# Second mixer of a two-block transformer kernel: rotary rows by transfers inside SBUF, indexer first, attention in pairs of heads with half product tiles between, gates by tanh

## The chip, the cores and the metric

One core of a Trainium2 chip runs the whole program in one launch. The time is the device time of one execution in microseconds. A core has TensorE (PE, matrix products into PSUM; PEld is its weight load), VectorE (DVE), ScalarE (ACT), GpSimd (POOL) and SyncE (SP, which only issues transfers here). PSUM has eight banks of 128 partitions by 512 fp32.

## The reference, cut to what matters

512 tokens of width 1024 in fp32 go through two blocks. The change touches only the mixer of the second block:

```python
def hybrid_mixer(xn, w_in, pool_w, pool_scale, w_pool_proj, w_attn_proj, w_out):
    proj = xn @ w_in
    u_pool, q, k, v, iq, ik, iw, gates = jnp.split(proj, cuts, axis=-1)
    pooled = multiscale_pool(u_pool)     # causal means over 2, 4, 8, 16 tokens, minus the token
    mixed = jnp.einsum('bsgc,gcd->bsgd', pooled, pool_w).reshape(B, S, POOL_WIDTH) * pool_scale
    y_pool = mixed @ w_pool_proj
    q, k, iq, ik = (rope_partial(a, pos) for a in (q, k, iq, ik))   # first 16 of 64 dims turned
    o = indexed_sparse_attention(q, k, v, iq, ik, iw)
    y_attn = o @ w_attn_proj
    g = jax.nn.sigmoid(gates).reshape(B, S, 2, D_MODEL)
    return (g[:, :, 0] * y_pool + g[:, :, 1] * y_attn) @ w_out

def indexed_sparse_attention(q, k, v, iq, ik, iw):     # per block row of 128 queries
    s = relu(iq . ik over 8 index heads of 64) / 8;  score = sum_h iw[h] / sqrt(8) * s[h]
    keep the 128 best causal keys of each query; softmax(q . k / 8) over them, times v, 8 heads of 64
```

After it come the conv FFN of the second block and the final norm, unchanged.

## The kernel before, in words

The program is written engine by engine (`nc.Block`), with semaphores; on each engine the order of the source is the order of the run. All products are made at fp32 accuracy out of fast matmuls: each weight unit of 128 x 2048 is split into a high part (ScalarE, `split`, L672) and a low part (`lo`: VectorE L1640, or GpSimd L585), and each product is three matmuls (L1153 to L1155). A product tile with 1024 inner values ("dense tile") is 24 matmuls of 512 columns, one with 512 inner values (`yp`, `ya`) is 12. Weight units pass through two slots in the order of `U`: SyncE loads unit u once unit u-2 has been parted, ScalarE splits it once TensorE has used unit u-2, VectorE or GpSimd then makes the low part, and TensorE waits for that (`weights_ready`).

PSUM tiles are handed out ahead of time by `Tiles.take`: each set of banks is a ring of its own (`GEMM` is banks 0 to 3, `AUX` 4 to 6, `HOLD` 7), and `wait_free` makes TensorE wait until the tile that had the bank before has been read.

The second mixer on TensorE: four pool tiles; the sum of squares for the norm (`rstd`, needed by everyone who reads a tile); q, k (column tiles), v (token tiles), iq, ikw, with after each pair of q, k, iq tiles two `swap` matmuls (L1530) that exchange the rotary halves of a copy of the tile (ScalarE L719 copies, GpSimd L643 multiplies by the cosines, VectorE L2164 and L2167 multiply by the sines and add); `project_pooled` (L1539) after the first q unit; `indexer(qt)` for block rows 1, 2, 3 (L1566, eight heads each of 64 rows; ScalarE L1062 takes the relu out of the bank, VectorE L2207 and L2209 weigh and sum) with gate units `gp` between; `yp` (products of the pooled branch, whose readers L1886 wait for the sigmoid gates, L1066). VectorE finds the 128 best keys by 16 rounds of eight maxima and a replacement (`top_rounds`, L2221, L2222): those of block rows 1 and 2 in one run after their indexer, those of 3 one per head in attention.

Attention then goes head by head over n = 0 to 31: `scores` (L1590), `turn_weights` of head n-1 (L1230), `weigh_values` of head n-2 (L1605), and in the first 16 steps a whole tile of the second gate (`ga`) at each odd n. On VectorE `at_maximum` (L2242, L2244) adds the mask and takes the row maximum; it may write `at_s[:, n % 2]` only when head n-2 has been turned. ScalarE takes the exponentials (L1087) and copies the turned weights (L1095). When the eight heads of a block row are done, `at_scaled` (VectorE L2251, L2254) divides, TensorE turns the rows, ScalarE (L1112) and VectorE (L2264, `at_lo`) make the high and low parts for `ya`. The attended rows of a block row (`o`) lie in bank 7 or bank 3, in turn. `ya`, `merged_hi`/`merged_lo` and `wo2` follow.

Of the kernel before, what the change touches and what calls it, by code (L numbers as in the profile page):

```python
# [8 lines left out]
ALU = mybir.AluOpType  # L9
# [45 lines left out]
for _g, _group in enumerate(VECTORS):  # L55
    _r = 0
    for _name, _n in _group:
# [5 lines left out]
          ("block_causal", P), ("chunk_of", CPT), ("rope_swap", P), ("pool_count", POOL_G * 16),  # L63
# [11 lines left out]
def shape_constants():  # L75
# [24 lines left out]
    c, s, swap = np.ones((P, S)), np.zeros((P, S)), np.zeros((P, P))  # L100
    for base in (0, HD):
        c[base:base + half] = c[base + half:base + rot] = cos
        s[base:base + half], s[base + half:base + rot] = -sin, sin
        for d in range(half):
            swap[base + d + half, base + d] = swap[base + d, base + d + half] = 1.0
    put("rope_cos", c)
    put("rope_sin", s)
    put("rope_swap", swap)
# [46 lines left out]
def program(nc, A, out):  # L155
# [10 lines left out]
    with ctx:  # L166
# [112 lines left out]
        pool_t, pooled = area(0, 3, 16 + S), area(1584, POOL_G, S)  # L279
        iq, ik = area(4096, 4, S), area(6144, S)  # L280
        at_q, at_k, at_v = area(R, 4, S), area(R + 2048, 4, S), area(R + 4096, TT, S)
# [57 lines left out]
        for name, n in [("sc", 3), ("conf", 2), ("ifa", 1), ("ml", 4), ("gate3", 4), ("y3", 1), ("gla", 4),  # L339
                        ("gate2", 4), ("y2", 1), ("gate0", 4), ("y0", 1), ("gate1", 4), ("y1", 1),  # L340
                        ("wo", 4), ("up1", FT), ("down1", FT // 2),
                        ("pool", 2), ("q", 2), ("k", 2), ("v", 2), ("iq", 2), ("ikw", 1), ("gp", 4), ("yp", 2),
# [17 lines left out]
        HEADS = TT * NH2  # L360

        def out_step(n):

            qt = (n - NH2 - 3) // NH2
            return qt if n >= NH2 + 3 and (n - NH2 - 3) % NH2 == 0 else None

        def ga_step(n):
            return n // 2 if n < 16 and n % 2 else None


# [62 lines left out]
        take("pl", AUX, POOL_G)  # L433
        take("rope", AUX, 13)
        take("iwT", AUX)
        take("idx", AUX, 3 * NH2)
        for name in ("gp", "yp"):
            take(name, GEMM, 8)
        take("ga", GEMM[:3], 8)
        take("o", HOLD + GEMM[3:], TT)  # L440
        for n in range(HEADS + 4):
            if n < HEADS:
                take("s", AUX)
            if 1 <= n <= HEADS:
                take("pt", AUX)
            if out_step(n) is not None:
                take("oT", AUX)
# [215 lines left out]
        def _(act):  # L663
# [349 lines left out]

            split(U["q"] + 1)
            rn = [0]

            def rotary():

                n = rn[0]
# [1318 lines left out]
```

## Time and profile before

| | us |
|---|---|
| median of 3 runs (lowest, highest) | 1784.95 (1782.24, 1785.29) |
| the profiled execution | 1785.4 |
| its span, first to last instruction | 1783.6 |
| TensorE busy, mean granted clock | 1675.6 (94%), 0.96 |
| VectorE, ScalarE, GpSimd busy | 950.0, 666.7, 325.3 |
| share of TensorE in the chain that ended last | 80% |

A row of a list or a timeline has the line, the engine, the operation, what it writes and reads, and its shape; "busy" on TensorE counts records that overlap, since matmuls are pipelined, so the step from one start to the next is the better price of a matmul. The granted clock is given as a share of 2.4 GHz.

### The profile page before, as it was taken

Reading aid. Unit: us, or ns where it says so; the run is one execution under the profiler, and the core shown is the slowest. Engines: PE = TensorE matmul, PEld = TensorE weight load, DVE = VectorE, ACT = ScalarE, POOL = GpSimd, SP = SyncE. Lnnn points to the kernel's source line nnn. Section 1 sums busy time; section 2 is a strip of 40 time slices with the busy share of each in tenths; the row PEclk is TensorE's granted clock in tenths of the full one; section 3 lists DMA queues with packets and bytes.
Section 4 is the critical chain, followed back from the end, with each engine's and each line's share of the span. In section 5 each row is a group of like instructions: output and inputs, shape, how many; then the busy total and the mean of one; then the engine's idle time right before and its main releaser. Section 6 shows DMA issues by size and latency. Waiting matters only on the chain.

```text
span 1783.6 us, 20062 instructions
## 1 busy us (share of the span) xinstructions
PE 1675.6 (94%) x7618; PEld 1333.8 (75%) x7618; DVE 950.0 (53%) x1274; ACT 666.7 (37%) x804; POOL 325.3 (18%) x150
## 2 busy tenths in 40 slices
PE   5899999989899799999998899998999999999997
PEld 4687678768777488888887668666767788888886
DVE  4549545436896644445333854664435455556333
ACT  2333353233223444444223422234353444544322
POOL 0320014224334011111000121343313211111000
PEclk8799999989999899999999999899999999999999
DMA  8323213206572133333222131221202233333221
GB/s 288 97 73 95 67 52 95 71 25 205 186 246 71 29 107 101 94 94 94 96 100 87 65 95 56 88 76 48 71 6 89 83 94 94 95 101 110 95 94 47
DMA packets 190956, 168.58 MB, mean 95 GB/s; under 512 B 9158, under 2 KB 180718, under 8 KB 190766
## 3 DMA queue, kind: packets, MB, share of 16 engines
q1 hardware_dynamic: 173485, 148.49, 27.0%
q10 hardware_dynamic: 16800, 16.83, 2.9%
q0 software_dynamic: 608, 2.41, 0.4%
q8 instruction: 42, 0.69, 0.2%
q14 instruction: 21, 0.16, 0.0%
HBM read 165.61 MB, written 2.10 MB: 94 GB/s over the span
## 4 chain that ended last, share of the span: by engine, by line
PE 80%; DVE 12%; issue 3%; ACT 2%; SPq 1%; DMA 1%; POOL 0%; DVEq 0%; ACTq 0%
PE bank L1153 23%; PE bank L1155 23%; PE bank L1154 23%; DVE work L1680 3%; PE bank L1178 1%; SPq L236 1%; DVE work L1743 1%; DVE w_lo L1640 1%; PE bank L1160 1%; PE bank L1161 1%; PE bank L1162 1%; PE bank L1230 1%; DVE tbuf L1652 1%; PE bank L1400 1%; PE bank L1566 1%
## 5 line engine op out<-in xcount | busy, mean ns | idle before, releaser
L1153 PE MATMUL bank<-h_hi,w_hi 128*128 128x512 f32 x1536 | 613.6, 399 | 29.4 <-DVE h_lo L1658 13.3
L1155 PE MATMUL bank<-h_hi,w_lo 128*128 128x512 f32 x1536 | 604.0, 393 | 0.0
L1154 PE MATMUL bank<-h_lo,w_hi 128*128 128x512 f32 x1536 | 603.9, 393 | 0.0
L1153 PEld LDWEIGHTS bank<-h_hi,w_hi 128*128 128x128 f32 x1536 | 291.8, 190 | 113.9 <-issue 37.5
L672 ACT ACTIVATE w_hi<-w_raw 128x2048 fp32r<-128x2048 f32 x131 | 250.2, 1910 | 303.3 <-PE bank L1155 234.3
L1640 DVE TENSOR_TENSOR w_lo<-w_raw,w_hi 128x2048 fp32r<-128x2048 f32 x88 | 202.5, 2301 | 262.6 <-ACT w_hi L672 262.3
L1155 PEld LDWEIGHTS bank<-h_hi,w_lo 128*128 128x128 f32 x1536 | 291.9, 190 | 62.0
L1154 PEld LDWEIGHTS bank<-h_lo,w_hi 128*128 128x128 f32 x1536 | 292.3, 190 | 59.9 <-issue 1.2
L585 POOL TENSOR_TENSOR w_lo<-w_raw,w_hi 128x2048 fp32r<-128x2048 f32 x43 | 204.1, 4746 | 467.3 <-ACT w_hi L672 467.3
L1153 PE MATMUL bank<-y_hi,w_hi 128*128 128x512 f32 x480 | 193.9, 404 | 19.4 <-DVE work L1886 8.5
L1154 PE MATMUL bank<-y_lo,w_hi 128*128 128x512 f32 x480 | 191.1, 398 | 0.0
L1155 PE MATMUL bank<-y_hi,w_lo 128*128 128x512 f32 x480 | 191.0, 398 | 0.0
L621 POOL TENSOR_TENSOR work<-work 128x512 f32 x44 | 56.8, 1292 | 468.0 <-ACT work L975 468.0
L1153 PEld LDWEIGHTS bank<-y_hi,w_hi 128*128 128x128 f32 x480 | 93.2, 194 | 42.7 <-DVE tbuf L1886 9.1
L1680 DVE SCALAR_TENSOR_TENSOR work<-work,small 128x256 f32<-128x256 f32 x154 | 108.8, 707 | 5.5
L1154 PEld LDWEIGHTS bank<-y_lo,w_hi 128*128 128x128 f32 x480 | 93.1, 194 | 19.8 <-issue 0.5
L1155 PEld LDWEIGHTS bank<-y_hi,w_lo 128*128 128x128 f32 x480 | 92.7, 193 | 20.0
L2067 DVE SCALAR_TENSOR_TENSOR work<-bank,par,work 128x511 f32<-128x511 f32 (+1 forms) x88 | 61.7, 743 | 71.1 <-ACT work L969 71.1
L969 ACT ACTIVATE work<-work,par 128x512 f32<-128x512 f32 x44 | 35.8, 815 | 97.8 <-DVE work L2056 97.8
L969 ACT ACTIVATE work<-bank,par 128x512 f32<-128x512 f32 x44 | 30.0, 683 | 105.2 <-PE bank L1155 105.2
L2067 DVE SCALAR_TENSOR_TENSOR work<-work,par 128x511 f32<-128x511 f32 (+1 forms) x88 | 61.9, 745 | 10.1 <-ACT work L969 10.1
L719 ACT ACTIVATE work<-bank,par 128x512 f32<-128x512 f32 x32 | 21.9, 686 | 116.8 <-PE bank L1155 116.8
(250 smaller groups left out, 1516.9 us busy)
## 6 DMA issues: line engine op xcount, KB each, us to landing
w_raw<-in_w_in SPq DMA_DIRECT2D x94, 512.0 KB, 4.6
w_raw<-in_ffn_w_up SPq DMA_DIRECT2D x44, 512.0 KB, 4.6
w_raw<-in_w_up SPq DMA_DIRECT2D x44, 512.0 KB, 4.5
work<-in_ada_w ACTq DMA_DIRECT2D x16, 1024.0 KB, 7.6
w_raw<-in_ffn_w_down SPq DMA_DIRECT2D x22, 512.0 KB, 3.9
w_raw<-in_w_down SPq DMA_DIRECT2D x22, 512.0 KB, 3.6
work<-in_ada_w SPq DMA_DIRECT2D x8, 1024.0 KB, 12.2
w_raw<-in_w_o SPq DMA_DIRECT2D x8, 512.0 KB, 4.0
```

The lines of the kernel that those rows point to most:

```text
L236: eng.dma_start(ada_place(n), A["ada_w"][0][:, n * 2 * P:(n + 1) * 2 * P].rearrange("(k p) n -> p k n", p=P))\
L585: pool.tensor_tensor(w_lo[u % 2][:, :], raw[u % 2][:, :], w_hi[u % 2][:, :].bitcast(FP32), ALU.subtract)\
L621: pool.tensor_tensor(work[:, bass.ds(i * (2 * S) + k * S, S)], cbuf[:, k, 0, :], cbuf[:, k, 1, :], ALU.mult).then_inc(sem("hid" + n), 1)
L672: act.activation(w_hi[u % 2][:, :], raw[u % 2][:, :], ACT.Copy).then_inc(hi_done, 1)
L719: release(act.activation(dst, src, func, **kw), t)
L969: act.activation(cbuf[:, k, part, :], src, ACT.Identity, scale=par[:, bass.ds(i * 2 + at, 1)], **kw).then_inc(sem("center" + n), 1)
L1153: pe.matmul(dst, w_hi[s][:, at:at + n], hi, start=first, stop=False)
L1154: pe.matmul(dst, w_hi[s][:, at:at + n], lo, start=False, stop=False)
L1155: return pe.matmul(dst, w_lo[s][:, at:at + n], hi, start=False, stop=last)
L1640: dve.tensor_tensor(w_lo[u % 2][:, :], raw[u % 2][:, :], w_hi[u % 2][:, :].bitcast(FP32), ALU.subtract)\
L1680: ins = dve.scalar_tensor_tensor(out=unit[:, 0, :], in0=unit[:, k, :], scalar=c_act[:, k:k + 1], in1=unit[:, 0, :], op0=ALU.mult, op1=ALU.add)
L2067: ins = dve.scalar_tensor_tensor(out=c[:, back:S], in0=src[:, 0:S - back], scalar=w, in1=c[:, back:S], op0=ALU.mult, op1=ALU.add)
```

## The change

It does five things, all in the second mixer.

1. **Rotary.** The swap matmuls, the copies to `tbuf` and GpSimd's products with the cosines go. VectorE reads each q, k, iq, ik tile out of its bank times `rstd` straight into place (`heads_out`). SyncE then gathers the 16 turning rows of each head into an area `turned` of 128 partitions x 512 by four transfers inside SBUF (`rotary_out`, 64 KB each read or written), VectorE turns all of them with four operations (`rotate`: two of 64 partitions, two of 128), and four transfers bring them back (`rotary_back`). Transfers stand in SyncE's queue among the weight loads.
2. **Order.** The order of units becomes pool, iq, ikw, q, k, v, gp, yp, ga, ya. All four pool tiles are read first; iq's tiles use the `GEMM` ring behind them. The indexer is cut into 12 pairs of heads, one after each of the tiles q1 to q3, k0 to k3, v0 to v3 and gp0; `project_pooled(g)` follows k0 to k3. `v` is read by ScalarE.
3. **Top-k spread.** Rounds of block rows 1 and 2 stand between index sums, the rest of 2 and all of 3 in attention steps 0 to 10.
4. **Attention in pairs.** A step m takes the scores of heads 2m and 2m+1, a half product tile, the turns of pair m-1, a half tile, the values of pair m-2. The 36 half tiles are gp 2 to 7, yp 0 to 7 (each one half), ga 0 to 7. Scores, turned weights and turned outputs share the ring of banks 3 to 6; `o` has bank 7 alone; gate and pool products use banks 0 to 2.
5. **Gates.** `tanh(x/2)` in the same table as the exponential; the readers add 1, and `wo2` is scaled by 0.5.

The core of the diff (helpers `ACT`/`POOL` order, tables of `take` and the copies of `split`/`lo` cut where the text above says them):

```diff
-        take("q", AUX[1:], 2)
-        for name, n in (("q", 2), ("k", 4), ("v", 4), ("iq", 4), ("ikw", 1)):
+        for name, n in (("iq", 4), ("ikw", 1), ("q", 4), ("k", 4), ("v", 4)):
             take(name, GEMM, n)
...
-        take("o", HOLD + GEMM[3:], TT)
+        for name in ("gp", "yp", "ga"):
+            take(name, GEMM[:3], 8)
+        take("o", HOLD, TT)
+        for m in range(PAIRS + 3):
+            if m < PAIRS:
+                take("s", GEMM[3:] + AUX, 2)
+            if 1 <= m <= PAIRS:
+                take("pt", GEMM[3:] + AUX, 2)
+            if m in O_TURNED_AT:
+                take("oT", GEMM[3:] + AUX)
...
+        O_TURNED_AT = (10, 11, 15, 18)
...  SyncE
+            rotary_out("iq", iq, T["iq"][3])
+            rotary_out("ik", ik, T["ikw"][0])
+            cols(U["k"], w2, KT, C_K, 2 * P)
+            rotary_back("iq", iq)
+            rotary_back("ik", ik)
...  TensorE
+                if p == 0:
+                    pe.wait_ge(sem("iq_back"), 64)
+                    pe.wait_ge(sem("ik_back"), 64)
...
+            for m in range(PAIRS + 3):
+                if m < PAIRS:
+                    scores(2 * m)
+                    scores(2 * m + 1)
+                if m <= PAIRS:
+                    fill_part(2 * m)
+                if 1 <= m <= PAIRS:
+                    turn_weights(2 * m - 2)
+                    turn_weights(2 * m - 1)
+                if m <= PAIRS:
+                    fill_part(2 * m + 1)
+                if 2 <= m <= PAIRS + 1:
+                    weigh_values(2 * m - 4)
+                    weigh_values(2 * m - 3)
+                if m == PAIRS + 1:
+                    fill_part(2 * m)
+                if m in O_TURNED_AT:
...
+                if m == PAIRS + 2:
+                    fill_part(2 * m - 1)
...  VectorE
+            for c in (2, 3):
+                heads_out("iq", c, iq, 1.0)
+            lo(U["q"])
+            t = T["ikw"][0]
+            wait_full(dve, t)
+            for b in (0, HD):
+                ins = dve.tensor_tensor(ik[b:b + HD, :], bank[t.bank][0:HD, :], rstd[0:HD, :], ALU.mult)
+            dve.wait_ge(sem("iw_rows"), 1)
+            release(ins, t)
+            dve.wait_ge(sem("rope_in"), 16)
+            rotate("iq")
+            lo(U["q"] + 1)
+            rotate("ik")
+            window_mean(3)
+            heads_out("q", 0, at_q, HEAD_SCALE)
...
+            ROUNDS_AT = {0: (2, 3), 1: (2, 3), 2: (2, 2), **{m: (3, 2) for m in range(3, 11)}}
+            for m in range(PAIRS + 3):
+                if m < PAIRS:
+                    at_maximum(2 * m)
+                    at_maximum(2 * m + 1)
+                if 7 <= m <= 10:
+                    for c in (2 * m - 14, 2 * m - 13):
+                        opened("yp", c, merged[:, c, :])
+                if m in ROUNDS_AT:
+                    top_rounds(*ROUNDS_AT[m])
+                if m >= 6 and (m - 6) % 4 == 0:
+                    at_scaled((m - 6) // 4)
+                if m in O_TURNED_AT:
+                    at_lo(O_TURNED_AT.index(m))
```

ScalarE in step m: the two exponentials, at even m the split of the weight unit due in two steps, the copies of the turned pair, one raw gate tile, one gate opened. GpSimd: the low parts from v's second unit on, and the scaling of each gate tile by `rstd`.

## Rows read from the trace of the kernel before

**Rows 1.** Busy time by stretch (x records), granted clock, transfers: indexer, attention, whole stage.
```profile
core 0: us, PE busy (x) PEld busy (x) DVE busy (x) ACT busy (x) POOL busy (x), PEclk, DMA share, GB/s
1130.80:1191.76 60.96, 60.81 (x241) 44.42 (x241) 49.67 (x124) 22.29 (x35) 28.66 (x12) 0.94 0.22 70
...
1221.70:1329.79 108.09, 100.82 (x513) 73.49 (x512) 49.95 (x158) 45.42 (x113) 28.50 (x12) 1.00 0.12 40
...
1008.16:1329.79 321.63, 300.36 (x1392) 226.38 (x1391) 171.59 (x365) 108.53 (x193) 87.99 (x41) 0.96 0.20 62
```

**Rows 2.** Waits of TensorE, 1008 to 1357: total, times, longest in us.
```profile
PE bank L1153 <- DVE work L1886: 4.9, 1, 4.9
PE bank L1539 <- DVEq L2157: 4.6, 1, 4.6
PE bank L1230 <- ACT work L1087: 4.4, 8, 1.3
...
PE bank L1530 <- ACT tbuf L1049: 1.9, 1, 1.9
PE bank L1566 <- DVE work L2167: 1.7, 1, 1.7
PE bank L1153 <- DVE y_lo L2264: 1.4, 1, 1.4
```

**Rows 3.** Timeline of TensorE around two swaps: start, length, instruction.
```profile
1105.22 2.04 PE L1530 MATMUL bank<-tbuf,cst 128*128 128x512 f32 x4
1106.69 0.79 PE L1153 MATMUL bank<-h_hi,w_hi 128*128 128x512 f32 x1
1107.32 0.40 PE L1154 MATMUL bank<-h_lo,w_hi 128*128 128x512 f32 x1
1107.55 0.40 PE L1155 MATMUL bank<-h_hi,w_lo 128*128 128x512 f32 x1
```

**Rows 4.** Timeline at the first index heads of block row 3, and their window.
```profile
1185.72 0.39 PE L1155 MATMUL bank<-h_hi,w_lo 128*128 128x512 f32 x1
1186.04 1.13 PE L1566 MATMUL bank<-work 64*128 64x512 f32 x4
...
1186.00:1187.00 1.00, 0.96 (x4) 0.49 (x5) 1.00 0.87 304
```

**Rows 5.** Timeline of TensorE, a head's scores of 512 columns.
```profile
1308.10 1.12 PE L1590 MATMUL bank<-work 64*128 64x512 f32 x2
1309.15 0.66 PE L1230 MATMUL bank<-cst,work 128*128 128x128 f32 x4
```

**Rows 6.** Timeline of VectorE in attention, 256 columns of scores, block row 3's rounds.
```profile
1253.16 0.42 DVE L2242 CUSTOM_DVE_ANT_0 work<-bank,work 128x256 f32<-128x256 f32 x1 [4.18 <-issue]
...
1253.70 0.68 DVE L2221 MAX8 small<-sq 128x8 f32<-128x512 f32 x1
...
1255.20 0.42 DVE L2242 CUSTOM_DVE_ANT_0 work<-bank,work 128x256 f32<-128x256 f32 x1
...
1257.49 0.69 DVE L2254 TENSOR_TENSOR tbuf<-bank,small 128x512 f32<-128x512 f32 x1
```

**Rows 7.** Timeline of VectorE: the first pool tile read, and four products out of banks.
```profile
1008.99 0.69 DVE L2133 TENSOR_TENSOR work<-bank,rstd 128x512 f32<-128x512 f32 x1 [4.47 <-issue]
...
1207.02 2.48 DVE L1886 SCALAR_TENSOR_TENSOR work<-bank,work 128x512 f32<-128x512 f32 x4 [12.79 <-ACT work L1066]
```

**Rows 8.** Transfers: issues, size, median us to landing; and two issues in SyncE's timeline.
```profile
work<-in_ada_w SPq DMA_DIRECT2D x8, 1024.0 KB, 12.2
...
w_raw<-in_w_in SPq DMA_DIRECT2D x1, 64.0 KB, 2.6
...
1004.55 0.92 SPq L485 DMA_DIRECT2D w_raw<-in_w_in  x2
```

**Rows 9.** Windows as in rows 1: a stretch with one wait of TensorE; after 4.9.
```profile
147.18:155.00 7.82, 6.09 (x51) 6.08 (x51) 7.82 (x11) 2.40 (x2) 0.00 (x0) 1.00 0.43 134
1206.83:1213.64 6.81, 5.78 (x14) 4.56 (x15) 2.77 (x5) 4.97 (x9) 2.72 (x1) 0.50 0.45 138
```

**Rows 10.** Group of GpSimd's low parts, 1008 to 1410: count, busy, mean ns.
```profile
L585 POOL TENSOR_TENSOR w_lo<-w_raw,w_hi 128x2048 fp32r<-128x2048 f32 x16 | 74.2, 4636 | 129.5 <-ACT w_hi L672 129.5
```

More of the change, by code:

```diff
@@ L99, in shape_constants @@
     cos, sin = np.cos(ang).T, np.sin(ang).T
[L100 to L108, printed above, removed]
+    row = np.arange(P)
+    dim, second = (row % 32) // 4, row >= HD
+    put("rope_cos", cos[dim])
+    put("rope_sin", np.where(second[:, None], -sin[dim], sin[dim]))
     t = np.arange(16)
@@ L357, in program, with fill @@
         GATE2_AFTER = {0: 0, 1: 1, 2: 2, 3: 3, 5: 5, 6: 6}
[L360 to L368, printed above, removed]
+        PAIRS = TT * NH2 // 2
+        INDEX_PAIRS = [(qt, h) for qt in range(1, TT) for h in range(0, NH2, 2)]
+        def fill(f):
+            if f < 12:
+                return "gp", 2 + f // 2, 4 * (f % 2)
+            if f < 20:
+                return "yp", f - 12, 0
+            return "ga", (f - 20) // 2, 4 * (f % 2)
+        O_TURNED_AT = (10, 11, 15, 18)
         READ_FIRST = (7, 0, 1, 2, 3, 4, 5, 6)
@@ L551, in _, with rows_between @@
             ffn_units("1", A["ffn_w_up"][0], A["ffn_w_down"][0])
-            for name, c0 in (("pool", C_POOL), ("q", C_Q), ("k", C_K), ("v", C_V), ("iq", C_IQ)):
-                column_units(name, w2, c0, 2)
-            cols(U["ikw"], w2, KT, C_IK, IKW)
-            column_units("gp", w2, C_GATE2)
+            def rows_between(name, X, gather):
+                for half in range(2):
+                    for hh in range(2):
+                        rows = X[hh * HD + half * 8:hh * HD + half * 8 + 8]
+                        at = half * HD + hh * 32
+                        if name == "ik":
+                            if gather:
+                                dst, src = turned[name][at:at + 32, :], rows.unsqueeze(1).broadcast_to([8, 4, S])
+                            else:
+                                dst, src = rows, turned[name][at:at + 32:4, :]
+                        else:
+                            dst, src = (turned[name][at:at + 32, :], rows) if gather else (rows, turned[name][at:at + 32, :])
+                        sp.dma_start(dst, src).then_inc(sem(f"{name}_{'out' if gather else 'back'}"), 16)
@@ L1114, in _ @@
+            open_gate("ga", KT - 1)
             split(U["ya"] + 1)
-            for cc in range(KT):
-                open_gate("ga", cc)
             split(U["ya"] + 2)
@@ L2226, in _ @@
             ch.link(dve.tensor_copy(masks[0], const("causal_qk")))
-            indexer(1)
-            top_rounds(1, 0, TOPK // 8)
-            indexer(2)
-            top_rounds(2, 0, TOPK // 8)
-            indexer(3)
-            gated("yp", first=True)
+            lo(U["iq"] + 1)
+            window_mean(0)
+            window_mean(1)
+            for c in range(2):
+                heads_out("iq", c, iq, 1.0)
+            lo(U["ikw"])
+            window_mean(2)
+            for c in (2, 3):
+                heads_out("iq", c, iq, 1.0)
@@ L2234, in at_maximum @@
+            for p in (8, 9, 10, 11):
+                index_sum(p)
+                top_rounds(2, 2)
             def at_maximum(n):
```

461 lines of the change are left out of this document (234 added, 227 removed).

## The prediction

> **What bounds the kernel now.** I read the page's busy table first, where TensorE stands far ahead of every other engine, then the windows by stage [rows 1]: the second mixer, up to its last product stage, runs from 1008.16 to 1329.79, 321.6 us; TensorE is busy for 300.4 of it at a mean granted clock of 0.96. VectorE has 171.6, ScalarE 108.5, GpSimd 88.0. So this is TensorE's queue, and a change can save there matmul time, waits, or slow clock. The list of waits says who ends them [rows 2]: 4.6 us for the pooled rows, 1.9 and 1.7 at the last rotary swap, 4.9 before the pool products (their banks are freed by products that wait for sigmoids), 4.4 in eight pieces for attention's exponentials, 1.4 for the last attended rows. The last rows say what a wait costs beyond itself: after the 4.9 the granted clock is 0.50 (1.2 GHz) for 6.8 us, while a stretch with one wait of 1.7 (147.2 to 148.9, busy 6.1 of 7.8) stayed at 1.00 (2.4 GHz) [rows 9]. Half of the busy time at 0.50 is lost, 2.9 us there; clock losses below are counted so, from the windows behind each wait.
>
> **Removed.** *Swaps.* Two swaps take TensorE from 1105.22 to 1106.69, and the next dense matmul lasts 0.63 instead of 0.23: 1.87 for two [rows 3]; 13 swaps are 12.2 us. A dense tile of 24 matmuls at that step of 0.23 (0.2275 over a whole tile) is 5.46, its half 2.73.
> *Waits of the projections.* The pooled rows are used 50 us later than they are ready: 4.6, plus 0.8 behind it for a weight part and some 3.1 of half clock. The swap's chain goes: 3.6, plus 1.4 of clock on the dense work behind it. Together 13.5.
> *Index heads.* The indexer's window of 60.96 us [rows 1] holds eight gate tiles (43.7) and 1.4 of slow clock in them: 24 heads cost 15.8. The window 1186.00 to 1187.00 holds four matmul records of 64 rows, two whole heads in 0.96 [rows 4]: neighbours sit in opposite halves of the array and run side by side. Only the first pair of a run can now, since three banks are then emptied one by one (15.8 for 24 is 0.66 a head). In pairs, with a dense tile in which ScalarE empties banks, I take 1.06, 0.85 and 0.63 a pair by width: 10.2 in all, 5.6 saved.
> *Pool products' wait.* The first half of them now stands between pairs; 4.9 and 2.9 of clock go: 7.8.
> *Attention's waits.* Two dense half tiles per pair now cover maximum and exponential: the 4.4 go, and 0.2.
> *Head pairs.* A lone head of 512 columns takes 1308.10 to 1309.15, 1.05 [rows 5]; two are 2.1 against 1.06 side by side. Saved 1.04 at 512, and, scaled with the columns, about 0.83, 0.63 and 0.42: four pairs of each, 11.7.
> Removed in all: 12.2+13.5+5.6+7.8+4.6+11.7 = 55.4.
>
> **Added.** *The first wait.* q's first tiles had banks of their own. Now iq takes the ring of four, and counted through the takes its first tile falls on bank 3, the pool tile that VectorE empties fourth. rstd is there at 1008.99, where VectorE starts the first; four such operations in a row take 2.48 [rows 7]. TensorE starts at 1011.6 instead of 1008.16: 3.4, and 2.2 of clock. 5.6.
> *Index transfers.* Before the first index pair stands: ikw tile read by VectorE (two operations, 1.4), gather of ik, the rotation of iq (2.9), a low part (2.3), the rotation of ik (2.9), transfer back. Counted from iq's first tile: ikw's tile full 27.3, read 28.7, iq turned 31.6, low part 33.9, ik turned 36.8. No row shows a transfer inside SBUF. The nearest is the one of 64 KB, 2.6 to landing; the longest on this queue is 12.2 [rows 8]. I take 2.6 because 64 KB is exactly the size, and 1.3 for the three issues ahead of the last (0.46 each): back at 40.7. TensorE asks at 38.8: 1.9 of wait, 0.9 of clock. The gather is covered by the rotation of iq and the low part; q's and k's come 25 us and more before use. Behind the waiting SyncE stand the weights of k, needed 15 us later.
> *VectorE in attention.* This I think the change overlooks. at_maximum(2m) waits until the weights of the pair before are turned, and that lies between the two half tiles of step m. From there VectorE needs 0.54 a head at 256 columns (start to start), about 0.67 at 384; a top-k round at 512 is 1.50, a product from a bank 0.69 (0.60 in a row), scaling with its reciprocal 1.0 [rows 6]. Two places hang on what it does next. (a) yp takes three banks, so the half tile after the turn at m=7, 8, 9 (yp 3, 5, 7) needs the product of yp 0, 2, 4 read in that same step: 1.2+0.7 after the turn, 1.45+0.7 at 384. Waits of 1.7, 1.9, 1.8. (b) "o" now has bank 7 alone, and the values of the next block row wait for at_scaled, which stands behind the rounds: at m=6 1.2+3.0+1.0 against a cover of 3.2, 2.0 of wait; at m=10 1.45+1.3+3.0+1.0 against 3.3, 3.5. At m=14 there are no rounds and the cover holds. Five waits, 10.9. Clock: the rows at hand show it kept after 1.7 and lost after 4.9 [rows 9]; I charge 4.5, between nothing and 8.5 (1.7 each).
> *More changes of kind.* From the last dense start before them to the index heads it is 0.32 instead of 0.23 [rows 4], and about as much on the way back: 0.16 a change with return. 28 more in attention, 12 in the projections: 6.4. The Trainium skill, "TensorEngine Tiling (Array Packing)", section "Tiling Modes", speaks against the change here: it says that switching the tiling mode drains the engine, and 64-row pairs between 128-row tiles switch each time. Taken as a full drain both ways (0.39 recorded less 0.23 step, twice) that would be 12.8, 6.4 us more than the sum.
> *The end.* The last gate half is copied, another gate is opened and the attended rows are copied on ScalarE, then VectorE takes the low part: 0.6+0.6+0.6+0.7 and signals, 2.75, against 1.4 now [rows 2] and the scaling of the last block row (1.0), which a half tile will hide. GpSimd's low parts of 4.64 [rows 10] for gate unit 3 and the first pool unit come 0.5 before they are asked for; each is queued behind a gate scaling. I put 0.8 on these and the value step at m=17: 1.1 in all.
> Added in all: 5.6+2.8+15.4+6.4+1.1 = 31.3.
>
> At nothing: DVE in the index stage. Its queue (17 tiles read, seven low parts, the rotations, the index sums, 16 rounds for block row 1 and 8 for 2) fits, since its rounds end at 122.5 and the first maximum is asked at 124; if that cover were gone, each late microsecond would be paid in full. GpSimd loses its 13 rotations and stands nowhere else on the path. From the "ya" products on nothing changes.
>
> **Sum.** 55.4 - 31.3 = 24.1 faster. The profiled execution took 1785.4 (span 1783.6), 0.45 over the median 1784.95. 1785.4 - 24.1 - 0.45 = 1760.9, said as **1761**.
>
> **Rivals.** *Nothing waits for VectorE in attention* (the banks are free in time, or other slack absorbs it): 15.4 come back, 1745.5. For: VectorE is busy 50 of 108 us in attention [rows 1]. Against: the order within a step is fixed.
> *The clock falls each time and longer, the waits lengthen*: five times 3.1 instead of 4.5 is 11, the transfer's wait 2 more: 1774.
> *The pairs don't run side by side* (so part of the change doesn't do what it says): 11.7 and 5.6 are lost: 1778. Against: the four records in 0.96 us [rows 4].
> *Slower, by the transfers:* out and back stand in series before the first index pair. With 12.2 for each, 19.2 are added: 1780. It decides from 14.6 us a transfer (24.1 = 2 x 12); at 18 each it is 1792. For: thirty-two rows of 2 KB go to as many partitions behind 1 MB of weights on one queue. Against: weights of 512 KB land in the order of 4 to 6 us.
> The skill's rule of the drain, as a mechanism of this kernel: 1767, inside the forecast's own range.
>
> **How the numbers follow.** Forecast 0.50, with its own range 1753 to 1769; nothing waits for VectorE 0.13; clock and longer waits 0.17; no pairs 0.08; transfers up to the neighbourhood of no change 0.04, beyond it 0.08. A difference under 0.2% (3.6 us) can't be told from no change in this kernel. Faster 0.50+0.13+0.17+0.08 = 0.88, of which I give 0.02 to "same", as couplings between five queues were judged: 0.86; same 0.06; slower 0.08. The range leaves out the transfers' slow end and the deepest gain: 1744 to 1778.
>
> **What would show it.** Swaps gone and TensorE's busy time in the second mixer about 20 us lower; its first wait of 3 to 4 us before iq, ended by a VectorE product out of a bank; a wait under 3 us at the first index pair ended by a transfer; 64-row records two at a time in attention; waits of about 2 us before the fourth, sixth and eighth pool products and before the first values of block rows 1 and 2 (2 and 3.5 us), all ended by VectorE; no wait for exponentials. The prediction is wrong if that first index wait is over 5 us, if waits appear in every step rather than in five, or if GpSimd's low parts end waits of more than 2 us.

## The result, and the profile after

The changed kernel takes 1757.9 us (1755.7 to 1759.9, four runs) against 1785.1 for the kernel before, measured beside it: a ratio of 0.984, 95% interval 0.983 to 0.986. The forecast was 1761, within 1744 to 1778. Its profiled execution took 1757.8 us, with a span of 1756.0.

The stage that the prediction works on ran from 1008.16 to 1329.79 before, 321.6 us [rows 1]. Windows of the changed kernel, first that stage, then the stretches around four of its waits; the columns are those of rows 1:

```profile
core 0: us, PE busy (x) PEld busy (x) DVE busy (x) ACT busy (x) POOL busy (x), PEclk, DMA share, GB/s
1007.02:1305.33 298.31, 274.39 (x1365) 216.43 (x1364) 160.82 (x359) 105.21 (x192) 75.62 (x28) 0.96 0.24 73
1050.90:1053.31 2.41, 0.00 (x2) 0.03 (x1) 2.16 (x6) 0.00 (x0) 0.00 (x0) 1.00 0.24 51
1053.31:1060.00 6.69, 6.69 (x32) 5.03 (x32) 4.76 (x7) 2.46 (x3) 0.00 (x0) 1.00 0.48 155
1183.04:1191.82 8.78, 6.35 (x21) 4.93 (x21) 2.19 (x5) 2.64 (x5) 3.36 (x2) 0.61 0.01 2
1215.44:1225.00 9.56, 7.48 (x38) 5.84 (x38) 5.27 (x14) 2.35 (x6) 0.00 (x0) 1.00 0.12 43
1228.54:1243.03 14.49, 7.39 (x26) 5.59 (x26) 7.45 (x10) 2.71 (x4) 4.50 (x1) 0.65 0.24 72
```

The stage is 298.3 us long, 23.3 less. TensorE's busy time in it fell by 26.0 (300.4 to 274.4); the mean granted clock is the same 0.96. So the gain is work taken out of TensorE's queue, and not waiting. The rest of the 27.6 between the two profiled executions lies outside: 1.1 ahead of the stage, where nothing was changed, and 3.1 behind it, where before has three stretches of 3.4 us at 0.50 and after has one.

TensorE's waits of over 1 us in the stage and just behind it, as total, times, longest; what answers to [rows 2]:

```profile
PE bank L1634 <- DVE tbuf L2327: 9.5, 2, 7.1
PE bank L1187 <- DVE work L2347: 6.2, 3, 2.2
PE bank L1187 <- DVE work L2171: 3.3, 1, 3.3
PE bank L1187 <- DVE h_lo L2033: 2.7, 1, 2.7
PE bank L1187 <- DVE y_lo L2337: 2.5, 1, 2.5
PE bank L1578 <- issue: 2.4, 1, 2.4
```

Of the old waits of over 1 us one is left: the one for the low part of the last attended rows, before the attention projection (L2337 is `at_lo`), was 1.4 and is 2.5. New are 3.3 at the first iq tile (L2171 reads the pool tile), 2.4 at the first index pair, three of about 2 before pool products (L2347 opens the tile whose bank they need), and two before the values of a new block row (L2327 is `at_scaled`). The fourth line, L2033, lies behind the stage and was there before too (2.7 at 1353.4). No line names ScalarE's exponentials. What ended the wait that is put down to "issue" shows in the same list, in the weight load of that matmul:

```profile
PEld bank L1578 <- DMA work<-work: 2.8, 1, 2.8
```

The pairs, on TensorE's timeline (start, length, instruction), to be set against the lone head of [rows 5]:

```profile
1249.94 1.13 PE L1619 MATMUL bank<-work 64*128 64x512 f32 x4
1251.00 0.50 PE L1187 MATMUL bank<-h_hi,w_hi 128*128 128x512 f32 x1
1251.34 0.39 PE L1188 MATMUL bank<-h_lo,w_hi 128*128 128x512 f32 x1
```

Two heads of 512 columns are over in 1.06 us, one took 1.05. The first dense matmul behind them takes 0.34 to the next start and not 0.23.

The longest wait, 7.10 us from 1228.54, on VectorE's timeline:

```profile
1227.06 1.29 DVE L2347 SCALAR_TENSOR_TENSOR work<-work,bank 128x512 f32<-128x512 f32 x2
1228.26 0.69 DVE L2246 MAX8 small<-sq 128x8 f32<-128x512 f32 x1
...
1230.58 0.67 DVE L2247 MATCH_REPLACE8 sq<-small,sq 128x512 f32<-128x512 f32 x1
1231.29 3.25 DVE L2250 TENSOR_SCALAR work<-sq 128x512 f32<-128x512 f32 x1
1234.57 0.20 DVE L2324 RECIPROCAL small<-small 128x8 f32<-128x8 f32 x1
1234.81 0.69 DVE L2327 TENSOR_TENSOR tbuf<-bank,small 128x512 f32<-128x512 f32 x1
```

And the one instruction on GpSimd's:

```profile
1229.75 4.50 POOL L624 TENSOR_TENSOR w_lo<-w_raw,w_hi 128x2048 fp32r<-128x2048 f32 x1 [17.67 <-ACT w_hi L707]
```

Products, two rounds and the scaling are there as the prediction has them. Between them stands an instruction that it left out: block row 3's mask (L2250), written once its 16 rounds are done. Before, the same operation took 0.43 us at 1283.80; here it takes 3.25, and it ends at 1234.54, 0.29 after GpSimd's low part of another weight tile (1229.75 + 4.50 = 1234.25).

SyncE's timeline with the transfers inside SBUF (L561; both lengths include waits):

```profile
1034.73 8.98 SPq L561 DMA_DIRECT2D work<-work  x8
...
1045.23 6.63 SPq L561 DMA_DIRECT2D work<-work  x8
```

VectorE's, turning ik, and TensorE's at the first index pair:

```profile
1046.23 1.41 DVE L2215 TENSOR_TENSOR work<-work,cst 64x512 f32<-64x512 f32 x2
...
1048.40 0.69 DVE L2217 TENSOR_TENSOR work<-work 128x512 f32<-128x512 f32 x1
```

```profile
1053.31 0.70 PE L1578 MATMUL bank<-work 64*128 64x256 f32 x4 [2.41 <-issue]
```

ik is turned at 1049.09. Its four issues run from 1049.17 to 1051.86, 0.69 from one start to the next. TensorE goes on at 1053.31, 1.45 after the last of them.

### The profile page after: what moved, and what is told of

It is laid out like the page before. It is cut to its first block, busy times and chain, and to the rows that moved or that the text cites. A ratio compares the mean times of both kernels' runs of the same rounds, so it can differ in the third digit from the quotient of the medians.

```text
span 1756.0 us, 19981 instructions
## 1 busy us (share of the span) xinstructions
PE 1644.7 (94%) x7592; PEld 1320.1 (75%) x7592; DVE 939.8 (54%) x1268; ACT 659.2 (38%) x796; POOL 312.9 (18%) x137
## 4 chain that ended last, share of the span: by engine, by line
PE 81%; DVE 12%; ACT 2%; SPq 2%; issue 2%; DMA 1%; POOL 0%; DVEq 0%; ACTq 0%
PE bank L1187 24%; PE bank L1189 23%; PE bank L1188 23%; DVE work L1721 4%; PE bank L1212 1%; PE bank L1634 1%; SPq L231 1%; PE bank L1194 1%; DVE work L1784 1%; PE bank L1196 1%; PE bank L1195 1%; DVE tbuf L1693 1%; PE bank L1438 1%; PE bank L1268 1%; DVE w_lo L1681 1%
## 5 line engine op out<-in xcount | busy, mean ns | idle before, releaser
L1681 DVE TENSOR_TENSOR w_lo<-w_raw,w_hi 128x2048 fp32r<-128x2048 f32 x86 | 198.0, 2302 | 266.2 <-ACT w_hi L707 265.9
L624 POOL TENSOR_TENSOR w_lo<-w_raw,w_hi 128x2048 fp32r<-128x2048 f32 x45 | 213.0, 4734 | 520.7 <-ACT w_hi L707 520.7
```

The costliest lines, as they stand in the source:

```text
L624: pool.tensor_tensor(w_lo[u % 2][:, :], raw[u % 2][:, :], w_hi[u % 2][:, :].bitcast(FP32), ALU.subtract)\
L1681: dve.tensor_tensor(w_lo[u % 2][:, :], raw[u % 2][:, :], w_hi[u % 2][:, :].bitcast(FP32), ALU.subtract)\
```

## The experiments

The theory: the projections and the matmul part of attention bring what the prediction says (swaps, pairs); the waits that remain are a matter of the order on VectorE and of one bank, and TensorE would take the time if they went. The rivals: VectorE (or GpSimd) is short of time there, so that a wait taken away comes back at the next place; and the pairs gain nothing by themselves.

**The mask out of the way.**

```diff
-                if rounds_done[qt] == TOPK // 8:
+                if rounds_done[qt] == TOPK // 8 and qt < 3:
...
                 if m >= 6 and (m - 6) % 4 == 0:
                     at_scaled((m - 6) // 4)
+                if m == 10:
+                    write_mask(3)
```

> The changed kernel with one operation of VectorE moved: the mask of block row 3 (one 128x512 comparison after the last round of step m=10) is written after at_scaled(1) instead of ahead of it. In the changed kernel TensorE waits 7.1 us at that place, where 3.5 were predicted; VectorE's mask took 3.25 us there, and 0.43 for the same shape in the kernel before, and it ended when GpSimd's low part ended (1234.3). Theory A (the mask is held while GpSimd works on its low part, and it alone is what the prediction left out): the wait falls by 3.3 to 3.8 us, the half clock behind it from 10.2 us to 3.4 or 6.8 us, total about 5 us less, 1753. Rival B (the rounds and products ahead are what was mis-sized, the mask's length only fills a time that VectorE has to wait anyway): the wait stays over 6 us and the time at 1758.

Measured 1756.5, ratio 0.984 [0.982, 0.986]. The profile has the wait at 3.8 and not 7.1, and the stage at 294.8 us, 3.5 shorter. So the mask is half of that wait. The stage in this profiled execution started 2.0 later than in the changed kernel's, where both run the same code; that hides most of it in the time as a whole, and the medians alone (1.4 apart, their runs overlapping) would not carry the verdict. The mask itself, now behind the scaling, started at 1234.39 and took 2.19: again to the end of GpSimd's low part (1236.29) and 0.29 more.

**The scaling ahead of everything else in its step.**

```diff
             for m in range(PAIRS + 3):
+                if m >= 6 and (m - 6) % 4 == 0:
+                    at_scaled((m - 6) // 4)
                 if m < PAIRS:
                     at_maximum(2 * m)
...
-                if m >= 6 and (m - 6) % 4 == 0:
-                    at_scaled((m - 6) // 4)
```

> The changed kernel with at_scaled as VectorE's first work of steps 6, 10, 14 and 18, ahead of the maxima, products, rounds and the mask; nothing else moves. Theory A (the values of the next block row wait for bank 7, and at_scaled is late only by the order of VectorE's own queue): the waits of 2.4 and 7.1 us at the first values of block rows 1 and 2 go, with the 17 us of half clock behind them (8.5 us of time, some of it shared with the product waits), about 16 us less: 1742, range 1738 to 1748. Rival B (VectorE is short of time as an engine): the same microseconds come back as waits at the next turns or maxima, and the time is within 4 us of 1758.

Measured 1746.7, ratio 0.979 [0.977, 0.981]. Both waits for L2327 are gone and one of 1.1 us is new: a turn now waits for the low part behind the mask. The stage takes 284.1 us, 14.3 less: 7.9 of waits, and 6.8 of half clock. The three stretches at 0.50 behind 1183 (6.8, 3.4 and 10.2 us long) are gone, the second though the product wait of 2.19 ahead of it is still there; one of 3.4 is new, 1.4 us behind the wait at the first index pair (1051.5).

**The pool products' tiles read ahead of the maxima.**

```diff
+                if 7 <= m <= 10:
+                    for c in (2 * m - 14, 2 * m - 13):
+                        opened("yp", c, merged[:, c, :])
                 if m < PAIRS:
                     at_maximum(2 * m)
                     at_maximum(2 * m + 1)
-                if 7 <= m <= 10:
-                    for c in (2 * m - 14, 2 * m - 13):
-                        opened("yp", c, merged[:, c, :])
```

> The changed kernel with the two pool products of steps 7 to 10 ahead of the step's maxima on VectorE; nothing else moves. Theory A (the half tiles yp 3, 5, 7 wait for a bank whose reader stands behind two maxima that wait for the turn of the same step): the three waits of 1.9, 2.2 and 2.1 us go, the one of 7.1 shrinks by 1.3, one stretch of half clock (3.4 us) goes: 9 us less, 1749. Rival B (the order is not the reason, the products are late because the gates are opened late): the waits stay, ended by ScalarE instead of VectorE, 1758.

Measured 1751.8, ratio 0.981 [0.979, 0.983]. The three waits are gone, the stage is 9.2 shorter, and one more stretch of 3.4 us at 0.50 stands behind it, at 1325. The wait of 7.1 did not shrink by the 1.3 that was expected: it is 7.07. The mask came earlier, at 1225.22, and took 4.46 instead of 3.25, again to 0.28 behind the end of GpSimd's low part (1229.40).

**Banks of their own for iq's first tiles.**

```diff
-        for name, n in (("iq", 4), ("ikw", 1), ("q", 4), ("k", 4), ("v", 4)):
+        take("iq", AUX[1:], 2)
+        for name, n in (("iq", 2), ("ikw", 1), ("q", 4), ("k", 4), ("v", 4)):
```

> The changed kernel with iq's first two tiles on banks 5 and 6, as q's were in the kernel before; the other tiles follow in the ring of four. Theory A (the first wait of 3.3 us is for the bank that VectorE empties fourth): it goes, and 1.7 us of half clock with it: 5 us less, 1753. Rival B (the index chain, not iq's tiles, decides when the first index pair can start): iq starts 3.3 us earlier but the wait at the first index pair grows from 2.4 by as much, and the time stays at 1757 to 1758. In between: VectorE's pool means come first in its queue and take part of it.

Measured 1754.9, ratio 0.983 [0.981, 0.985]. The first wait is gone, no other took its place, and the stage is 3.3 shorter. The half clock did not go with it: the 3.4 us that lay behind this wait now lie behind the next one, at the first index pair (1049.4 to 1052.8).

**The three together** (scaling, then products, then maxima, then rounds; and iq's banks, which are 5 and 6, not 4 and 5 as the expectation says).

> In each round of attention VectorE divides by the sums first, then opens the pool products' tiles, then the row maxima and top-k rounds; and iq's first two tiles take banks 4 and 5. The three single edits took 11.2 (scaled first), 6.1 (products first) and 3.0 us (iq's banks) off the changed kernel's 1757.9. Theory A (each wait for VectorE in attention is a matter of its order, and the engine has time to spare there): the edits add up, save for the clock's share that the first already has: 1738, range 1734 to 1742, and no wait for L2324 to L2347's tiles is left between 1180 and 1300 us, but one of about 1 us for the turn behind the mask. Theory B (VectorE is short of time there, and a wait that is taken away comes back later, before the attention projection): about 1747, like scaled first alone.

Measured 1736.7 (1733.9 to 1737.2), ratio 0.972 [0.970, 0.975]; the first theory's number. Its waits of TensorE from 1000 to 1340, and the windows of its stage and of the first index pair:

```profile
PE bank L1188 <- DVE h_lo L2034: 2.7, 1, 2.7
PE bank L1188 <- DVE y_lo L2338: 2.5, 1, 2.5
PE bank L1579 <- issue: 2.4, 1, 2.4
PE bank L1269 <- DVEq L2341: 1.1, 1, 1.1
PE bank L1188 <- ACT work L755: 0.5, 1, 0.5
```

```profile
1007.77:1279.69 271.92, 265.42 (x1366) 210.34 (x1365) 162.38 (x359) 104.45 (x192) 75.82 (x28) 0.99 0.27 80
1046.60:1056.00 9.40, 7.02 (x25) 5.28 (x26) 6.65 (x11) 2.46 (x3) 0.00 (x0) 0.82 0.39 122
```

VectorE does the same work (162.4 us busy against 160.8) in 26.4 us less of stage. It had the time; the order and one bank were against it. Of the 26.4, 17.4 are waits and 8.5 half clock.

**The pairs pulled apart.** Against the kernel with the three together:

```diff
                     scores(2 * m)
-                    scores(2 * m + 1)
                 if m <= PAIRS:
                     fill_part(2 * m)
+                if m < PAIRS:
+                    scores(2 * m + 1)
```

> The kernel both_iq with the second head's scores of each round issued after the first half tile instead of right behind the first head's: the heads are turned and weighed in pairs still, but no two scores stand side by side. Theory A (two 64-row matmuls on the two halves of the array overlap, as the prediction's 11.7 us for attention has it): 11.7 us slower than both_iq, and up to 2.6 more for 16 more switches of pattern at 0.16, so 12 to 14 us. Theory B (the lone head's time was no more than its wait for the exponential, and the pair gains nothing by itself): within 3 us of both_iq.

Measured 1748.7, ratio 0.980 [0.977, 0.982], 12.0 slower. One of the two heads of a round now looks like this:

```profile
1246.27 0.39 PE L1189 MATMUL bank<-h_lo,w_hi 128*128 128x512 f32 x1
1246.50 0.39 PE L1190 MATMUL bank<-h_hi,w_lo 128*128 128x512 f32 x1
1246.82 1.12 PE L1620 MATMUL bank<-work 64*128 64x512 f32 x2
1247.87 0.88 PE L1269 MATMUL bank<-cst,work 128*128 128x128 f32 x6
```

A lone head takes 1.05 again, for every width what it took before. Summed from each record's start to the next one's, the 64 score matmuls take 23.5 us here and 11.9 in the kernel with pairs: 11.6, where the prediction has 11.7. The last dense matmul ahead of the head takes 0.32 instead of 0.23. The stage is 13.1 longer: these 11.6, 1.5 on dense matmuls and 0.9 on turns, less 1.0 of waits. The pairs' gain is the pairs' own.

**No half tile between turns and values.**

```diff
+                if m <= PAIRS:
+                    fill_part(2 * m + 1)
                 if 1 <= m <= PAIRS:
                     turn_weights(2 * m - 2)
                     turn_weights(2 * m - 1)
-                if m <= PAIRS:
-                    fill_part(2 * m + 1)
```

> The kernel both_iq with both half product tiles of a round ahead of the turns, so that the values' products follow the turns with nothing between. Theory A (the half tile between turns and values covers ScalarE's copy of the turned weights): a wait of some 1 to 1.5 us in each of 16 rounds, 15 to 25 us slower and more where the clock falls. Theory B (ScalarE's copies are fast enough, and a switch between product tiles and small matmuls costs 0.16 us): 16 times 2 switches less, up to 5 us faster than both_iq.

Measured 1751.8, ratio 0.981 [0.979, 0.984], 15.1 slower: the size that the first theory names, though not by its mechanism. The values of a round belong to the pair turned a round earlier, so they don't wait for the copies just begun. What waits is the next scores, whose banks VectorE and ScalarE must empty first: three of the four pairs of 512 take 1.15, 1.26 and 1.85 us instead of 1.06, and all scores 6.0 more in sum. One wait of 3.0 for a gate bank behind ScalarE's queue, one of 1.7 for a copy of turned weights and 4.5 of half clock come on top. The half tile between is needed, but for the banks of the next step.

**The swaps back.** The changed kernel with this matmul in 13 places, behind each tile of q, k and v (and the index pair that follows it) and behind the second pooling gate. Like a swap of before (L1530) it is one matmul of 512 columns, not four of 128 as the expectation says:

```diff
+                pe.matmul(bank[7][:, :], const("ident"), x[:, 0, :], start=True, stop=True)
```

> The changed kernel with 13 matmuls of 512 fp32 columns against the identity put among the projections, into a bank that nobody reads and with nobody waiting for them: the bare price of the swaps that the change removed. Theory A (each costs what four 128-column ones took in the trace of before, 0.94 us): 12.2 us slower than the changed kernel, 1770. Theory B (they fall partly into TensorE's waits in that stretch, of which there is one of 2.4 us): 8 to 10 us slower.

Measured 1767.9, ratio 0.989 [0.987, 0.992]: 10.0 over the changed kernel by medians, 10.4 in the stage. One of them on the timeline:

```profile
1062.75 0.70 PE L1578 MATMUL bank<-work 64*128 64x256 f32 x4
1063.38 1.12 PE L1591 MATMUL bank<-x,cst 128*128 128x512 f32 x2
1063.95 0.80 PE L1187 MATMUL bank<-h_hi,w_hi 128*128 128x512 f32 x1
1064.58 0.40 PE L1188 MATMUL bank<-h_lo,w_hi 128*128 128x512 f32 x1
```

It costs 0.57 itself here, and the dense matmul behind it takes 0.63, where one behind a pair takes 0.34. Summed over the records of the stage, the 13 take 7.6 themselves and the matmuls beside them 3.5 more: 11.2, of which 0.8 disappear in the wait at the first index pair (1.6 left of 2.4). The first theory has 12.2; the 10.0 of the medians are the upper end of the second.

**The mask in another form.** Against the kernel with the three together:

```diff
-                    ch.link(dve.tensor_scalar(masks[qt], acc, 0.5 * TAKEN, NEG, ALU.is_gt, ALU.mult))
+                    ch.link(dve.scalar_tensor_tensor(out=masks[qt], in0=acc, scalar=0.5 * TAKEN, in1=small[:, 254:255].broadcast_to([P, N]),
+                                                     op0=ALU.is_gt, op1=ALU.mult))
```

> The kernel both_iq with each attention mask written by one scalar_tensor_tensor (its second operand a column of the constant, broadcast) in place of the tensor_scalar of fp32 SBUF to SBUF. Theory A (the tensor_scalar of 128x512, 0.43 us by itself, took 3.25 to 4.46 us because it could not go on before GpSimd's low part, 4.5 us of another tile, had ended, and the form whose neighbours MAX8 and the subtractions from PSUM keep their 0.69 us is not held up): the op takes about 0.7 us, the turn's wait of 1.1 us goes, 1.1 us faster than both_iq, 1735.5. Theory B (any VectorE operation between two SBUF tiles is slowed while GpSimd works): the op still takes over 2 us and nothing changes.

Measured 1735.3, ratio 0.971 [0.969, 0.972], not to be told from the kernel without it; that the first theory has 1735.5 is chance, as the operation shows. VectorE's timeline, and GpSimd's:

```profile
1216.28 0.68 DVE L2249 MATCH_REPLACE8 sq<-small,sq 128x512 f32<-128x512 f32 x1
1216.99 4.81 DVE L2252 SCALAR_TENSOR_TENSOR work<-sq,small 128x512 f32<-128x512 f32 x1
1221.83 0.69 DVE L2340 TENSOR_TENSOR y_lo<-bank,y_hi 128x512 fp32r<-128x512 f32 x1
```

```profile
1216.67 4.58 POOL L625 TENSOR_TENSOR w_lo<-w_raw,w_hi 128x2048 fp32r<-128x2048 f32 x1 [11.39 <-ACT w_hi L708]
```

The first theory fell: 4.81 us where it has 0.7. The new form is held too, until 0.55 after GpSimd's end, and the turn waits 1.4 instead of 1.1. The rival in its wide form, that any operation between SBUF tiles is slowed, fell as well: the maxima and replacements among GpSimd's instruction keep their 0.69 and 0.68 (in the changed kernel 1229.77 to 1231.25 lies wholly in it). In the changed kernel and in every experiment the last mask met a low part of GpSimd, and it ends 0.28 to 0.55 us after it. The Trainium skill, "SBUF — State Buffer", section "SBUF: two separate sides", says that VectorE operations in a two-port mode, or (against a GpSimd operation that reads SBUF) with two SBUF inputs, share an exclusive port pair with GpSimd: whichever starts first has it for the whole instruction, and the other stands still. The trace agrees: it is an order, not a slower rate. By that rule the new form was a poor choice, since it has two SBUF inputs, and the kernel before had shown as much: ahead of the stage a SCALAR_TENSOR_TENSOR of 128x256 with two inputs in SBUF (L1680 there, 0.49 us otherwise) takes 4.6 to 4.9 eight times where it starts with a low part of GpSimd, or just behind its start, as at 434.9 and 445.4. A form with a single input outside the two-port mode wasn't tried.

**Every index pair one projection tile later.** Against the kernel with the three together:

```diff
-            for c in (1, 2, 3):
-                column_tile("q", c)
-                index_scores(c - 1)
+            column_tile("q", 1)
+            for c in (2, 3):
+                column_tile("q", c)
+                index_scores(c - 2)
...
-                index_scores(3 + c)
+                index_scores(2 + c)
...
-                index_scores(7 + n)
+                index_scores(6 + n)
```

with ScalarE's and VectorE's reads moved alike, the first rounds of block row 1 moved behind them, and the banks of the pooled rows dealt out one pair earlier.

> The kernel both_iq with every pair of index heads one projection tile later on all engines (the first behind the third tile of q, the last behind the second tile of the pooling gates). Theory A (the 2.4 us wait at the first pair is for the rows that come back from the rotary transfers, which land less than 3 us after it was asked for): the wait goes, with 1.7 us of half clock that follows it, and q's tile of 5.9 us covers it: 4 us faster than both_iq, 1732.5. Theory B (the top-k rounds, now begun a tile later, hold up VectorE in attention instead, or a later pair waits for its bank): the gain is given back, 1735 to 1740.

Measured 1735.4 (0.971 [0.970, 0.972]), 1.3 below the kernel without it by medians and inside both spreads; the stage is 272.2 us against 271.9. The wait at the first pair is gone. A new one stands in attention, on TensorE's timeline; the second fence is GpSimd's:

```profile
1140.84 0.49 PE L1621 MATMUL bank<-work 64*128 64x128 f32 x4
1143.50 0.79 PE L1188 MATMUL bank<-h_hi,w_hi 128*128 128x512 f32 x1 [2.17 <-POOL w_lo L625]
```

```profile
1137.60 1.30 POOL L679 TENSOR_TENSOR work<-work,rstd 128x512 f32<-128x512 f32 x1 [6.46 <-ACT work L755]
1138.86 4.58 POOL L625 TENSOR_TENSOR w_lo<-w_raw,w_hi 128x2048 fp32r<-128x2048 f32 x1
```

The low part of the next gate unit stands in GpSimd's queue behind a gate's scaling and comes 2.2 us late. The half clock of 3.4 us follows it there. Before, the earlier wait had paid for this one. Neither theory named GpSimd; the gain was given back as the second has it.

**Both last edits together.**

> The kernel both_iq with the later index pairs and the masks' other form together. Theory A: both gains, 5 us faster than both_iq, 1731.5. Theory B: as shift alone, or slower.

Measured 1736.2, ratio 0.971 [0.970, 0.973]. The two waits of the last two experiments are both there (2.2 and 1.4), and nothing is gained.

**The gates' function.** The changed kernel with the sigmoid itself in the gates. The readers still add 1, so the gates' values are not the reference's; the run prices the function alone:

```diff
-                act.activation(gates[:, cc, :], gates[:, cc, :], ACT.Tanh, scale=0.5)
+                act.activation(gates[:, cc, :], gates[:, cc, :], ACT.Sigmoid)
```

> The changed kernel with the sigmoid in place of tanh in its 16 gate tiles, and the products still multiplied by one plus it, so that the gates' values are not the reference's: the price of the sigmoid among the exponentials. Theory A (the table loads that it brings, 1.28 us each, fall in ScalarE's idle time of 3 to 5 us a round, as the prediction had ScalarE's load at nothing): within 3 us of the changed kernel. Theory B (the load for the next exponential lies on the way from the row maximum to the turn): up to 1.3 us in each of the 15 rounds with a gate, 10 to 20 us slower.

Measured 1758.4, ratio 0.984 [0.982, 0.985], the changed kernel's time. From 1130 to 1310 ScalarE loads tables 23 times more than the changed kernel, which has no load there:

```profile
L1103 ACT ACT_TABLE_LOAD x12 | 15.4, 1283 | 0.2
L1108 ACT ACT_TABLE_LOAD x11 | 14.1, 1283 | 0.2
```

That is 29.5 us on ScalarE, and TensorE's waits are the same to 0.02 us. A load stands right behind the gate, ahead of the exponential's wait for the maximum (1149.31 and 1.28 long, the exponential at 1151.95 after 1.36 of idle time). Behind the loads of this kind 0.03 to 2.5 us of idle time are left. So tanh is worth nothing here.

## Why the prediction was right, and where its steps were off

The time came out 3 us from the forecast. The table sets its sum against the stage. The measured column is worked out from all TensorE records of both stages: from each record's start to the next one's, without the waits, with half of what ran at clock 0.50 counted as clock, and grouped by line. The prediction's 12.2 for the swaps is split into their own time (0.735 each, 9.6) and the slower dense matmul behind them (2.6).

| step | predicted | measured, before and after |
|---|---|---|
| swaps themselves | -9.6 | -10.2 (10.2 to 0) |
| heads of attention in pairs | -11.7 | -12.4 (24.1 to 11.7) |
| index heads in pairs | -5.6 | -3.0 (13.2 to 10.2) |
| dense tiles: changes of kind, less those behind swaps | +3.8 | +4.7 (207.1 to 211.8) |
| waits | -1.2 (18.5 removed, 17.3 added) | +2.9 (21.0 to 23.9) |
| clock | +0.2 (7.4 and 7.6) | +0.3 (9.9 to 10.2) |
| turns, values, pooled rows | 0 | -5.5 (36.1 to 30.6) |
| sum | -24.1 | -23.2 |

*Swaps and pairs* held, and both are shown by taking them back (11.2 for the 13 matmuls with what they do to the next; 11.6 for the pairs).

*Index heads.* The term that was mis-sized is the price of a head before. The granted clock is 0.50 from 1128.31 to 1138.55, and so for the first 7.75 us of the window 1130.80 to 1191.76. The prediction took off the 1.4 of clock that fall on the gate tiles; 2.4 more fall on the first eight heads (1130.83 to 1135.67). So 15.8 for 24 heads holds 2.4 of slow clock, and the heads alone are 13.2. Those 2.4 did go, but they belong to the row of the clock. After is right: 1.06, 0.85 and 0.63 a pair.

*Clock.* That 7.4 and 7.6 come out at 9.9 and 10.2 is the same error of 2.5 on both sides, so the row's fit is luck. Before, it is the 2.4 just named. After, attention has 8.5 for 4.5, the first wait 1.7 for 2.2, the index transfers nothing for 0.9.

*The first wait*: 3.3 against 3.4, ended by L2171 as told, with 1.7 of clock against 2.2. Taking the bank away took the wait away.

*Index transfers*: 2.4 of wait against 1.9, and no half clock behind it (windows above: 1.00 to 1060.00). The issue was put at 0.46 from weight transfers [rows 8]; inside SBUF it is 0.69 here, so that the last transfer is issued 0.8 later than put. Its landing makes up for 0.5 of it: 2.1 from the start of its issue at the latest, against 2.6. The chain ahead was 2 us longer than worked out, ik turned 38.75 after iq's first tile and not 36.8, but TensorE asked 1.8 later too (40.6 and not 38.8).

*VectorE in attention.* The five waits are where they were named, on the engine and line named: 2.4, 1.9, 2.2, 2.1 and 7.1 against 2.0, 1.7, 1.9, 1.8 and 3.5. The fifth is the mis-sized term: the chain left out the mask, and with it 3.3 us that its price alone (0.43) would not have given. The trace of before had the warning: a mask of 256 columns took 2.38 us at 1153.07, ending 0.15 after a GpSimd low part. Clock there was 8.5 against 4.5, which is the upper bound that the prediction names. The rival "nothing waits for VectorE", 1745.5, is what an edit to the order brings (1746.7 for the scaling alone, 1736.7 with the rest).

*Changes of kind.* Into a pair the last dense matmul takes 0.32, out of it 0.34, against 0.23: 0.20 a change with return where 0.16 was charged, 8.0 for 40. The Trainium skill's rule of the drain ("TensorEngine Tiling (Array Packing)", "Tiling Modes") has the right sign. Taken as the full drain both ways that the prediction worked out, 12.8, it is too dear by the rows.

*The last wait*: 2.5 against 2.75. GpSimd's low parts ended no wait in the changed kernel; their half microsecond of room is what the later index pairs used up.

*Not foreseen*: the turns, values and pooled rows take 5.5 less. Turns went from 13.0 to 10.2 for the same 100 matmuls, values from 19.2 to 18.1, the pooled rows from 3.7 to 2.3. The records show where: inside a run a turn steps 0.109 us and a value 0.112 in both kernels, and the difference lies at the ends of the runs. Before, 36 runs of turns began at 0.16, nearly all behind a lone head; after, 20 begin at 0.109, and with the pairs pulled apart, a lone head in front again, at 0.153. The last value ahead of a head of scores steps 0.21, 20 times before and 11 times after. What the pooled rows save was not looked into further. Nor was the 3.1 behind the stage, which hangs on where the clock fell.

So the good number has two halves. Four rows fit within 1 us, one of them (the clock) by two equal errors. The other three miss by 2.6 (index heads), 4.1 (waits) and 5.5 the other way (turns and the rest), which cancel but for 1.2. With the 2.4 put where they belong, the misses are 4.1 for the waits, 2.5 for the clock behind them and the 5.5. The waits were right in place and cause wherever the prediction names one, and the mask is the piece that it left out; that the sum comes within 3 us is luck.

## What to carry to other kernels

Follow the chain of an engine's whole step, with every instruction in it, also the one that comes only once, at the end of a loop; here it was half of the longest wait. Where two engines work side by side, look for an operation of one that ends just behind an instruction of the other: that is an order. Another form with two inputs in SBUF did not buy it off, and moving the mask helped only by taking it off the way of what TensorE needed next. When waits on an engine with time to spare hang on its order, put first what the busiest engine needs soonest; two such moves and one change of banks brought as much as three quarters of the change itself (21.2 beside 27.2 us), while a further move only uncovered the next wait.

## What the runs showed of the hardware

- VectorE's mask between SBUF tiles stands still while GpSimd subtracts between SBUF tiles: 0.43 us alone (512 columns), 2.19 to 4.54 when they meet (4.81 in the other form), always ending 0.28 to 0.55 after GpSimd does; the one of 256 columns in the kernel before ends 0.15 after. Maxima and replacements are not held.
- The same shows ahead of the stage, and in both directions. In the changed kernel a SCALAR_TENSOR_TENSOR of 128x256 with two inputs in SBUF, 0.49 us otherwise, takes 4.7 to 4.9 eight times between 433 and 560, each time ending about 0.3 after a low part of GpSimd; and GpSimd's low part, 4.6 otherwise, takes 7.0 at 410.7 and 6.7 at 540.5, where it meets VectorE's subtractions between SBUF tiles at their usual 0.68.
- TensorE's clock after a wait can't be told from the wait's length alone. In one execution it stayed at 1.00 (2.4 GHz) after waits of 2.41, 1.90 and 2.08 us and fell to 0.50 (1.2 GHz) after 2.43 for 6.8 us and after 2.19 for 3.4. With the first wait of the stage taken away, the 2.4 at the index pair is followed by the 3.4 at half clock that it had been spared. With the scaling moved, the same wait of 2.19 is followed by none.
- A transfer of 64 KB inside SBUF, between 8 partitions and 32, keeps SyncE 0.69 us from one start to the next; the row for a weight transfer gave 0.46.
- Two matmuls of 64 rows in opposite halves of the array take the time of one: 1.06 for two of 512 columns, 1.05 for one.
- ScalarE's table loads of 1.28 us between a gate and the next exponential cost nothing where ScalarE idles for a maximum; 0.03 to 2.5 us of that idle time were left behind the load.
